# Differential attention: three score regions, alternating row halves, and turned weights through one bank

## The chip, the cores and the metric

One core of a Trainium2 chip runs the whole program. The metric is device time in microseconds (us), the median of several executions. The engines are TensorE (PE for matmuls, PEld for weight loads), VectorE (DVE), ScalarE (ACT), GpSimd (POOL) and SyncE (SP), each with an instruction stream of its own.

## The reference, cut to what matters

Two transformer blocks run one after the other on 512 tokens of width 1024, in float32. The change is in the second block's differential attention: 4 heads, each with two maps of 64 channels, 512 queries, 768 keys (256 of context) and 128 value channels.

```python
def diff_attention(q, k_all, v_all, lam):
    s = jnp.einsum('bhmqd,bhmkd->bhmqk', q, k_all).astype(jnp.float32) * ATTN_SCALE
    pr = jax.nn.softmax(s, axis=-1)
    a = pr[:, :, 0] - lam * pr[:, :, 1]
    return jnp.einsum('bhqk,bhke->bhqe', a.astype(v_all.dtype), v_all)
```

Each head's output is then divided by its root mean square (diff_post).

## The kernel before, in words

The program is a list of phases, and each phase gives every engine a piece of code; phases follow on each engine without a common stop. `diff_attention` comes after `diff_projection` and before `diff_post`. PSUM has eight banks of 512 float32 columns.

The work is cut into 16 **units** (head h, block i of 128 queries), in one loop over u on each engine; the code's order is the order of each engine's queue, and semaphores join the queues.

- TensorE, `scores(pe, u, m)`: the scores of map m, 128x768, are one 512-column and one 256-column matmul. Map 0 lies in partitions 0 to 63 of Q and K, map 1 in 64 to 127, so each uses one half of the array's rows. Map 0 is issued whole, then map 1 (lines 2331 and 2332). Map m has banks 2m and 2m+1, so the scores of unit u wait for the exponential of unit u-1 of the same map (`raised`). In the trace a float32 matmul is two instructions.
- VectorE takes each map's row maximum (line 2380), negates it in a second instruction (2381) and signals `maxed`. After the maxima of unit u it finishes unit u-1: reciprocal of the second map's sum (2387), the ratio (2388), and the difference of the two maps over 768 columns (2389), which signals `ready`.
- ScalarE raises each map (2411), with the row sum read out by a second instruction, and signals `raised`; then it copies (2419) the turned weights of unit u-2 to the table PT and signals `copied`.
- TensorE, `turns(pe, u)`: six transposes of 128x128 (2340) turn the weights of unit u-2 into banks 4 and 5; they wait for `ready` and for the copy of the unit before. `values(pe, h, keys)`: once four units of a head are copied, six key blocks of 512 columns (2349) add up in bank 6, two blocks in each of three units; the head's values begin at u = 4h+6. VectorE takes the result (`take`, 2401), ScalarE squares it (2429), and `diff_sum` (318 and 2445) adds up columns in bank 7.
- While the last units drain, `latents` (2465) fills TensorE with matmuls of the next projection: "context" and "first" at u = 16, "last" after the loop. Then come diff_sum(2), values(3) with all six blocks, and the next phase's products (2135).

Of the kernel before, what the change touches and what calls it, by code (L numbers as in the profile page):

```python
# [16 lines left out]
ALU = mybir.AluOpType  # L17
ACT = mybir.ActivationFunctionType
AX_X = mybir.AxisListType.X

P = 128
D = 1024
KD = D // P
S = 512
# [106 lines left out]
def view(M, off, *dims):  # L131
    n = int(np.prod(dims))
    v = M[:, off:off + n]
    if len(dims) == 1:
        return v
    names = "abcde"[:len(dims)]
    return v.rearrange("p (" + " ".join(names) + ") -> p " + " ".join(names),
                       **{c: d for c, d in zip(names[1:], dims[1:])})
# [1151 lines left out]
class Seven:  # L1290
# [68 lines left out]
    def copy(self, act, u):  # L1359
        self.wait_product(act, u, 1)  # L1360
        if u >= 1:
            self.wait_added(act, u - 1, "u2")
        act.activation(self.CP[:, 0, :], self.bank(1), ACT.Copy).then_inc(self.copied, 1)
# [944 lines left out]
def diff_attention(k):  # L2308


    M = k.M
    Q, K, V = view(M, D_Q, 4, S), view(M, D_K, 4, T_ALL), view(M, D_V, TT, 512)
    MIX, SQ = view(M, A_MIX, KD, S), view(M, D_SQ, 4, S)
    PT, PR = view(M, D_PT, 2, TT, S), view(M, D_P, 3, 2, T_ALL)
    top, total, ratio, floor = view(M, O_SML, 2, 2), view(M, O_SML + 4, 4, 2, 4), view(M, O_SML + 36, 2), view(M, O_SML + 40, 4, 4)
    units = [(h, i) for h in range(4) for i in range(4)]
    N = len(units)
    scored, maxed, raised, ready, turned, copied, valued, taken = (
        k.attention[x] for x in ("scored", "maxed", "raised", "ready", "turned", "copied", "valued", "taken"))
    m0, t0, u0, h0 = (k.attention_count[x] for x in ("scored", "turned", "copied", "valued"))  # L2320
    score = lambda m: k.psum[:, 1024 * m:1024 * m + T_ALL]
    TURN, VALUE = 4, 6
    k.latents = k.sem("latents")
    k.diffpost = squared, summed, rooted, inverted = [k.sem(f"diffpost_{x}") for x in ("squared", "summed", "rooted", "inverted")]

    def scores(pe, u, m):
        h, i = units[u]
        if u >= 1:
            pe.wait_ge(raised, m0 + 2 * u - 1 + m)
        r = slice(64 * m, 64 * m + 64)  # L2330
        pe.matmul(k.bank[2 * m], Q[r, h, i * P:(i + 1) * P], K[r, h, 0:512], start=True, stop=True)  # L2331
        pe.matmul(k.bank[2 * m + 1][:, :256], Q[r, h, i * P:(i + 1) * P], K[r, h, 512:768], start=True,
                  stop=True).then_inc(scored, 1)

    def turns(pe, u):
        pe.wait_ge(ready, u + 1)
        if u >= 1:
            pe.wait_ge(copied, u0 + u)
        for j in range(TT):
            mm = pe.transpose(k.bank[TURN + j // 4][:, (j % 4) * P:(j % 4 + 1) * P], PR[:, u % 3, 0, j * P:(j + 1) * P], k.ident)  # L2340
        mm.then_inc(turned, 1)

    def values(pe, h, keys):
        if 0 in keys:
            pe.wait_ge(copied, u0 + 4 * h + 4)
            if h >= 1:
                pe.wait_ge(taken, h0 + h)
        for j in keys:
            mm = pe.matmul(k.bank[VALUE], V[:, j, h * P:(h + 1) * P], PT[:, h % 2, j, :], start=j == 0, stop=j == TT - 1)  # L2349
        if TT - 1 in keys:  # L2350
            mm.then_inc(valued, 1)

    def tensor(k, pe):
        for u in range(N + 2):
            if u < N:
                scores(pe, u, 0)
            h, step = (u - 2) // 4 - 1, (u - 2) % 4
            if u < N:
                scores(pe, u, 1)
            if h >= 0 and step < 3:  # L2360
                values(pe, h, (2 * step, 2 * step + 1))
            if u == N:
                latents(k, pe, "context")
            if u >= 2:
                turns(pe, u - 2)
            if u % 4 == 3 and u >= 11:
                diff_sum(k, pe, u // 4 - 2)
            if u == N:
                latents(k, pe, "first")
        latents(k, pe, "last")  # L2370
        diff_sum(k, pe, 2)
        values(pe, 3, range(TT))

    def vector(k, dve):
        for u in range(N + 1):
            if u < N:
                for m in range(2):
                    t = top[:, u % 2, m:m + 1]
                    dve.wait_ge(scored, m0 + 2 * u + m + 1)
                    k.dve.link(dve.tensor_reduce(t, score(m), AX_X, ALU.max))  # L2380
                    dve.tensor_scalar(t, t, -1.0, None, ALU.mult).then_inc(maxed, 1)
            if u >= 1:
                v = u - 1
                h, i = units[v]
                r, pr = ratio[:, v % 2:v % 2 + 1], PR[:, v % 3]
                dve.wait_ge(raised, m0 + 2 * v + 2)
                k.dve.link(dve.reciprocal(r, total[:, h, 1, i:i + 1]))
                k.dve.link(dve.scalar_tensor_tensor(out=r, in0=total[:, h, 0, i:i + 1], scalar=k.lam, in1=r, op0=ALU.mult, op1=ALU.mult))
                dve.scalar_tensor_tensor(out=pr[:, 0, :], in0=pr[:, 1, :], scalar=r, in1=pr[:, 0, :],
                                         op0=ALU.mult, op1=ALU.subtract).then_inc(ready, 1)  # L2390
                if i == 3:
                    k.dve.link(dve.tensor_scalar(floor[:, h, :], total[:, h, 0, :], SUBLN_EPS * P / D, None, ALU.mult))
                    k.dve.link(dve.tensor_tensor(floor[:, h, :], floor[:, h, :], total[:, h, 0, :], ALU.mult))
                if u % 4 == 1 and u >= 9:
                    take(dve, u // 4 - 2)
        take(dve, 2)
        take(dve, 3)

    def take(dve, h):
        dve.wait_ge(valued, h0 + h + 1)  # L2400
        dve.tensor_copy(MIX[:, 4 + h, :], k.bank[VALUE]).then_inc(taken, 1)

    def scalar(k, act):
        for u in range(N + 2):
            if u < N:
                if u >= 3:
                    act.wait_ge(turned, t0 + u - 2)
                h, i = units[u]
                for m in range(2):
                    act.wait_ge(maxed, m0 + 2 * u + m + 1)  # L2410
                    act.activation(PR[:, u % 3, m, :], score(m), ACT.Exp, bias=top[:, u % 2, m:m + 1],
                                   accum_out=total[:, h, m, i:i + 1]).then_inc(raised, 1)
            if u >= 2:
                v = u - 2
                h, i = units[v]
                act.wait_ge(turned, t0 + v + 1)
                if h >= 2:
                    act.wait_ge(valued, h0 + h - 1)
                act.activation(PT[:, h % 2, :, i * P:(i + 1) * P],
                               k.psum[:, 512 * TURN:512 * TURN + T_ALL].rearrange("p (j q) -> p j q", q=P),  # L2420
                               ACT.Copy).then_inc(copied, 1)
                if u % 4 == 2 and u >= 10:
                    square(act, u // 4 - 2)
        square(act, 2)
        square(act, 3)

    def square(act, h):
        act.wait_ge(taken, h0 + h + 1)
        act.activation(SQ[:, h, :], MIX[:, 4 + h, :], ACT.Square).then_inc(squared, 1)

    ph = Phase("diff_attention", tensor=tensor, vector=vector, scalar=scalar)
    ph.soft = True
    return ph
# [15 lines left out]
def latents(k, pe, what):  # L2449

    W, A, C = view(k.M, A_MIX, KD, 160), view(k.M, A_A, KD, S), k.ctxT
    raised, m0 = k.attention["raised"], k.attention_count["raised"]
    if what == "gate":
        pe.wait_ge(raised, m0 + 32)
        block_feature(pe, k.bank[2][0:96, :], W, 64, 96, lambda q: A[:, q, :], KD).then_inc(k.latents, 1)
        return
    if what == "context":
        pe.wait_ge(raised, m0 + 31)  # L2460
    bank, rhs, chunks = {"context": (k.bank[1][:, :NC_CTX], C, range(KD)), "first": (k.bank[0], A, range(0, KD // 2)),
                         "last": (k.bank[0], A, range(KD // 2, KD))}[what]
    for q in chunks:
        for r, c0 in ((0, 0), (64, 32)):
            mm = pe.matmul(bank[r:r + 32, :], W[:, q, c0:c0 + 32], rhs[:, q, :], start=q == 0, stop=q == KD - 1)
    if what == "last":
        mm.then_inc(k.latents, 1)
# [1103 lines left out]
```

## Time and profile before

| | us |
|---|---|
| median of 3 runs | 2581.02 |
| lowest, highest run | 2575.54, 2581.93 |
| span of the profiled execution, first to last instruction | 2573.8 |
| first score matmul | 1507.03 |
| first matmul of the next phase (products) | 1603.52 |

The profiled execution has no device time beside its span: the three runs are other executions, and their median lies 7.2 us above the span. The profile gives each instruction's start from the start of the span. PEclk is the granted TensorE clock as a share of 2.4 GHz: 0.50 is its lower level, 1.2 GHz. Matmuls are pipelined, so a matmul's duration includes its drain, and the distance of two starts says how fast they follow.

### The profile page before, as it was taken

To read this page: it belongs to the slowest core of one execution; us is meant where nothing else is said; L and a number is where in the kernel's file an instruction comes from. 1 tells how busy PE (TensorE), PEld (TensorE's weight loads), DVE (VectorE), ACT (ScalarE), POOL (GpSimd) and SP (SyncE) were. 2 spreads that over 40 slices of the span, in tenths; PEclk is the share of its full clock that TensorE was granted. 3 is DMA by queue.
4 is the path that set the end of the run, shared out by engine and by line. 5 is a ranking of instruction groups with operands and counts; after the bars stand their busy time and mean duration, and the time that the engine had idled before them with its cause. 6 is when DMAs were issued, how large, how long until landed. Compare 5 with 4: busy or idle time off the path is not lost.

```text
span 2573.8 us, 45719 instructions
## 1 busy us (share of the span) xinstructions
PE 2460.1 (96%) x19672; PEld 1922.6 (75%) x19672; DVE 1364.2 (53%) x2613; ACT 519.6 (20%) x1046; POOL 127.6 (5%) x106
## 2 busy tenths in 40 slices
PE   8999999999999999999998999998889898999998
PEld 5945888888686548888885664557888746888887
DVE  5636555533454426555435465566666436787633
ACT  2121010000003421010001034224444223112101
POOL 0000000000000000000000000002222200000000
PEclk9999999999999999999999989999999998999999
DMA  5323332233222023232234210400000033223132
GB/s 171 123 84 129 99 98 67 78 90 111 67 66 67 1 66 119 78 98 81 75 90 145 74 33 2 120 1 3 4 4 4 4 112 117 67 98 99 52 84 78
DMA packets 222176, 190.31 MB, mean 74 GB/s; under 512 B 8711, under 2 KB 220072, under 8 KB 221976
## 3 DMA queue, kind: packets, MB, share of 16 engines
q1 hardware_dynamic: 221682, 187.29, 23.6%
q8 instruction: 157, 2.57, 0.4%
q14 instruction: 43, 0.35, 0.0%
q10 hardware_dynamic: 294, 0.09, 0.0%
HBM read 185.25 MB, written 2.10 MB: 73 GB/s over the span
## 4 chain that ended last, share of the span: by engine, by line
PE 90%; DVE 5%; issue 2%; ACT 1%; SPq 1%; POOL 1%; DMA 0%; POOLq 0%; DVEq 0%; ACTq 0%
PE psum L1676 31%; PE psum L1897 14%; PE psum L517 7%; PE psum L2780 6%; PE psum L1353 5%; PE psum L1349 4%; PE psum L1136 4%; PE psum L3335 2%; PE psum L1072 1%; PE psum L2787 1%; PE psum L2331 1%; PE psum L2349 1%; PE psum L539 1%; POOL sbuf L432 1%; PE psum L1115 1%
## 5 line engine op out<-in xcount | busy, mean ns | idle before, releaser
L1676 PE MATMUL psum<-sbuf 128*128 128x256 f32 x3696 | 806.0, 381 | 3.5 <-DVE sbuf L481 1.9
L1676 PEld LDWEIGHTS psum<-sbuf 128*128 128x128 f32 x3696 | 707.1, 191 | 102.1 <-issue 3.1
L1897 PE MATMUL psum<-sbuf 128*128 128x256 f32 x1716 | 370.9, 379 | 0.0
L1897 PEld LDWEIGHTS psum<-sbuf 128*128 128x128 f32 x1716 | 326.0, 190 | 44.3
L1760 DVE TENSOR_TENSOR sbuf<-sbuf,psum 128x256 f32<-128x256 f32 x462 | 177.6, 416 | 202.0 <-PE psum L1676 200.8
L2780 PE MATMUL psum<-sbuf 64*64 64x64 f32 (+1 forms) x5952 | 209.0, 223 | 29.9 <-DVE sbuf L3172 10.2
L2780 PEld LDWEIGHTS psum<-sbuf 64*64 64x64 f32 x5952 | 194.4, 136 | 43.5 <-issue 23.4
L517 PE MATMUL psum<-sbuf 128*128 128x512 f32 (+3 forms) x560 | 205.5, 524 | 0.3 <-issue 0.3
L517 PEld LDWEIGHTS psum<-sbuf 128*128 128x128 f32 (+2 forms) x560 | 104.5, 188 | 93.0 <-issue 87.0
L1933 DVE TENSOR_TENSOR sbuf<-sbuf,psum 128x256 f32<-128x256 f32 x84 | 34.0, 418 | 216.5 <-PE psum L1897 216.1
L432 POOL TENSOR_TENSOR sbuf<-sbuf 128x512 f32<-128x512 f32 x30 | 37.8, 1280 | 1885.9 <-DVE sbuf L418 1885.7
L1353 PE MATMUL psum<-sbuf 128*128 128x256 f32 (+2 forms) x536 | 122.3, 389 | 0.0
L1353 PEld LDWEIGHTS psum<-sbuf 128*128 128x128 f32 x536 | 99.1, 190 | 23.5 <-issue 3.2
L1349 PEld LDWEIGHTS psum<-sbuf 128*128 128x128 f32 x1008 | 113.8, 192 | 2.8 <-issue 2.4
L1136 PE MATMUL psum<-sbuf 128*128 128x512 f32 x256 | 114.3, 595 | 0.6 <-DVEq L622 0.6
L1349 PE MATMUL psum<-sbuf 128*128 128x128 f32 x1008 | 113.8, 275 | 0.0
L1696 ACT ACTIVATE sbuf<-sbuf 128x512 f32<-128x512 f32 x44 | 27.7, 630 | 399.9 <-DVE sbuf L1760 399.9
L3237 POOL TENSOR_TENSOR sbuf<-sbuf 128x512 f32<-128x512 f32 x60 | 75.0, 1274 | 547.4 <-DVE sbuf L3161 517.0
L1411 DVE TENSOR_TENSOR sbuf<-sbuf,psum 128x256 f32<-128x256 f32 (+1 forms) x119 | 53.4, 450 | 70.9 <-PE psum L1353 39.5
L1746 DVE TENSOR_TENSOR sbuf<-sbuf 128x512 f32<-128x512 f32 x66 | 44.4, 689 | 81.2 <-PE psum L1676 67.2
L1136 PEld LDWEIGHTS psum<-sbuf 128*128 128x128 f32 x256 | 46.8, 190 | 51.9 <-issue 51.2
L3172 DVE TENSOR_TENSOR sbuf<-sbuf,psum 128x256 f32<-128x256 f32 x120 | 47.5, 402 | 64.0 <-PE psum L2780 63.8
(281 smaller groups left out, 2653.7 us busy)
## 6 DMA issues: line engine op xcount, KB each, us to landing
sbuf<-in_w_mod_dram SPq DMA_DIRECT2D x24, 1024.0 KB, 5.1
sbuf<-in_w_ffn_gate_dram SPq DMA_DIRECT2D x22, 1024.0 KB, 5.5
sbuf<-in_w_ffn_up_dram SPq DMA_DIRECT2D x22, 1024.0 KB, 7.8
sbuf<-in_w_ffn_down_dram SPq DMA_DIRECT2D x32, 704.0 KB, 5.9
sbuf<-in_w_up_dram SPq DMA_DIRECT2D x22, 1024.0 KB, 7.4
sbuf<-in_w_out_dram SPq DMA_DIRECT2D x12, 1024.0 KB, 6.7
sbuf<-in_w_in_dram SPq DMA_DIRECT2D x12, 1024.0 KB, 5.6
sbuf<-in_w_down_dram SPq DMA_DIRECT2D x16, 704.0 KB, 6.4
```

The source lines that it names most:

```text
L432: pool.tensor_tensor(k.H[:, c, :], k.H[:, c, :], j.tmp[:, n % 3, :], ALU.add).then_inc(j.moved, 1)
L517: mm = pe.matmul(bank, w[:, q, c0:c0 + m], rhs(k0 + q), start=start and q == 0, stop=stop and q == kc - 1)
L1136: mm = pe.matmul(bank_of(b), tiles[b // 2][:, q, (b % 2) * P:(b % 2) * P + P], MIX[:, q, :], start=q == 0, stop=q == KD - 1)
L1349: mm = pe.matmul(self.bank(p)[:, t * P:(t + 1) * P], x[:, q, :], w[:, q, :], start=q == 0, stop=q == 3)
L1353: mm = pe.matmul(self.bank(p)[:, c0:c1], w[:, q, :], x[:, q, :], start=q == 0, stop=q == 3)
L1411: dve.tensor_tensor(out, base, flat(self.bank(p)), ALU.add).then_inc(self.added, 1)
L1676: mm = pe.matmul(bank, w[:, q, :], rhs[:, q, :], start=q == 0, stop=q == 3)
L1760: dve.tensor_tensor(out, base, bank_of(u, p, t), ALU.add).then_inc(s["added"], 1)
L1897: mm = pe.matmul(bank_of(g, p), wt[:, q, :], rhs_of[p][:, q, :], start=q == 0, stop=q == UNITS - 1)
L2780: mm = pe.matmul(out[h], lhsT[h], rhs[h], start=start, stop=stop)
L3237: pool.tensor_tensor(split(LOFF[lv]), split(GB[g % 2][:, :, 0, :]), both_level(lv), ALU.mult).then_inc(sems["loff"], 1)
L3335: mm = pe.matmul(block_bank(b), tiles[b // 2][:, q, (b % 2) * P:(b % 2 + 1) * P], MIX[:, q, :], start=q == order(b)[0], stop=q == order(b) ...
```

## The change

- **Regions.** Six banks in three pairs are handed round: the 2u+m-th map takes pair (2u+m) mod 3. One wait, for the first exponential of unit u-1, goes ahead of both maps' scores, and the four matmuls alternate: both maps' 512 columns, then both maps' 256.
- **Negation.** The maximum is negated in the reduction (`negate=True`); the second instruction and the wait between go.
- **Turned weights.** They pass through bank 7 alone, in two parts: early (key blocks 0 to 3) and late (4 and 5). Each part waits on TensorE for the copy of the part before. ScalarE copies the late part of unit u-3 between the two exponentials of unit u, and the early part of u-2 behind the second.
- **SBUF.** First maps take four buffers, second maps two (six of 768 columns, as before).
- **Shifts.** The values of a head begin one unit later (u = 4h+7), `take` and `square` too; diff_sum(0) to diff_sum(2) all come behind values(3).

```diff
@@ -2311,38 +2311,44 @@
     M = k.M
     Q, K, V = view(M, D_Q, 4, S), view(M, D_K, 4, T_ALL), view(M, D_V, TT, 512)
     MIX, SQ = view(M, A_MIX, KD, S), view(M, D_SQ, 4, S)
-    PT, PR = view(M, D_PT, 2, TT, S), view(M, D_P, 3, 2, T_ALL)
+    PT, PR = view(M, D_PT, 2, TT, S), view(M, D_P, 6, T_ALL)
+    raised_map = lambda u, m: PR[:, u % 4 if m == 0 else 4 + u % 2, :]
...
-    score = lambda m: k.psum[:, 1024 * m:1024 * m + T_ALL]
-    TURN, VALUE = 4, 6
+    region = lambda u, m: 2 * ((2 * u + m) % 3)
+    score = lambda u, m: k.psum[:, 512 * region(u, m):512 * region(u, m) + T_ALL]
+    TURN, VALUE = 7, 6
+    early, late = range(0, 4), range(4, TT)
+    of_turn = lambda u, part: 2 * u + (1 if part is early else 2)
...
 
-    def scores(pe, u, m):
+    def scores(pe, u):
         h, i = units[u]
         if u >= 1:
-            pe.wait_ge(raised, m0 + 2 * u - 1 + m)
-        r = slice(64 * m, 64 * m + 64)
-        pe.matmul(k.bank[2 * m], Q[r, h, i * P:(i + 1) * P], K[r, h, 0:512], start=True, stop=True)
-        pe.matmul(k.bank[2 * m + 1][:, :256], Q[r, h, i * P:(i + 1) * P], K[r, h, 512:768], start=True,
-                  stop=True).then_inc(scored, 1)
-
-    def turns(pe, u):
+            pe.wait_ge(raised, m0 + 2 * u - 1)
+        for keys in (slice(0, 512), slice(512, 768)):
+            for m in range(2):
+                r = slice(64 * m, 64 * m + 64)
+                mm = pe.matmul(score(u, m)[:, keys], Q[r, h, i * P:(i + 1) * P], K[r, h, keys], start=True, stop=True)
+                if keys.stop == T_ALL:
+                    mm.then_inc(scored, 1)
+
+    def turns(pe, u, part):
         pe.wait_ge(ready, u + 1)
-        if u >= 1:
-            pe.wait_ge(copied, u0 + u)
-        for j in range(TT):
-            mm = pe.transpose(k.bank[TURN + j // 4][:, (j % 4) * P:(j % 4 + 1) * P], PR[:, u % 3, 0, j * P:(j + 1) * P], k.ident)
+        if of_turn(u, part) >= 2:
+            pe.wait_ge(copied, u0 + of_turn(u, part) - 1)
+        for j in part:
+            mm = pe.transpose(k.bank[TURN][:, (j - part[0]) * P:(j - part[0] + 1) * P], raised_map(u, 0)[:, j * P:(j + 1) * P], k.ident)
         mm.then_inc(turned, 1)
 
     def values(pe, h, keys):
         if 0 in keys:
-            pe.wait_ge(copied, u0 + 4 * h + 4)
+            pe.wait_ge(copied, u0 + of_turn(4 * h + 3, late))
             if h >= 1:
                 pe.wait_ge(taken, h0 + h)
         for j in keys:
@@ -2352,24 +2358,24 @@
 
     def tensor(k, pe):
         for u in range(N + 2):
+            h, step = (u - 3) // 4 - 1, (u - 3) % 4
             if u < N:
-                scores(pe, u, 0)
-            h, step = (u - 2) // 4 - 1, (u - 2) % 4
-            if u < N:
-                scores(pe, u, 1)
+                scores(pe, u)
+            if u >= 3:
+                turns(pe, u - 3, late)
+            if u == N:
+                latents(k, pe, "context")
             if h >= 0 and step < 3:
                 values(pe, h, (2 * step, 2 * step + 1))
-            if u == N:
-                latents(k, pe, "context")
             if u >= 2:
-                turns(pe, u - 2)
-            if u % 4 == 3 and u >= 11:
-                diff_sum(k, pe, u // 4 - 2)
+                turns(pe, u - 2, early)
             if u == N:
                 latents(k, pe, "first")
         latents(k, pe, "last")
-        diff_sum(k, pe, 2)
+        turns(pe, N - 1, late)
         values(pe, 3, range(TT))
+        for h in range(3):
+            diff_sum(k, pe, h)
 
     def vector(k, dve):
         for u in range(N + 1):
@@ -2377,21 +2383,19 @@
                 for m in range(2):
                     t = top[:, u % 2, m:m + 1]
                     dve.wait_ge(scored, m0 + 2 * u + m + 1)
-                    k.dve.link(dve.tensor_reduce(t, score(m), AX_X, ALU.max))
-                    dve.tensor_scalar(t, t, -1.0, None, ALU.mult).then_inc(maxed, 1)
+                    dve.tensor_reduce(t, score(u, m), AX_X, ALU.max, negate=True).then_inc(maxed, 1)
             if u >= 1:
                 v = u - 1
                 h, i = units[v]
...
...
-                if u % 4 == 1 and u >= 9:
+                if u % 4 == 2 and u >= 10:
                     take(dve, u // 4 - 2)
         take(dve, 2)
         take(dve, 3)
@@ -2401,26 +2405,36 @@
         dve.tensor_copy(MIX[:, 4 + h, :], k.bank[VALUE]).then_inc(taken, 1)
 
     def scalar(k, act):
+        def raise_map(u, m):
+            h, i = units[u]
+            act.wait_ge(maxed, m0 + 2 * u + m + 1)
+            if m == 0 and u >= 4:
+                act.wait_ge(turned, t0 + of_turn(u - 4, late))
+            elif m == 1 and u >= 2:
+                act.wait_ge(ready, u - 1)
+            act.activation(raised_map(u, m), score(u, m), ACT.Exp, bias=top[:, u % 2, m:m + 1],
+                           accum_out=total[:, h, m, i:i + 1]).then_inc(raised, 1)
+
+        def copy(v, part):
+            h, i = units[v]
+            act.wait_ge(turned, t0 + of_turn(v, part))
+            if h >= 2:
+                act.wait_ge(valued, h0 + h - 1)
+            act.activation(PT[:, h % 2, part[0]:part[-1] + 1, i * P:(i + 1) * P],
+                           k.bank[TURN][:, 0:len(part) * P].rearrange("p (j q) -> p j q", q=P), ACT.Copy).then_inc(copied, 1)
+
         for u in range(N + 2):
             if u < N:
-                if u >= 3:
-                    act.wait_ge(turned, t0 + u - 2)
-                h, i = units[u]
-                for m in range(2):
-                    act.wait_ge(maxed, m0 + 2 * u + m + 1)
-                    act.activation(PR[:, u % 3, m, :], score(m), ACT.Exp, bias=top[:, u % 2, m:m + 1],
-                                   accum_out=total[:, h, m, i:i + 1]).then_inc(raised, 1)
+                raise_map(u, 0)
+            if u >= 3:
+                copy(u - 3, late)
+            if u < N:
+                raise_map(u, 1)
             if u >= 2:
-                v = u - 2
-                h, i = units[v]
-                act.wait_ge(turned, t0 + v + 1)
-                if h >= 2:
-                    act.wait_ge(valued, h0 + h - 1)
-                act.activation(PT[:, h % 2, :, i * P:(i + 1) * P],
-                               k.psum[:, 512 * TURN:512 * TURN + T_ALL].rearrange("p (j q) -> p j q", q=P),
-                               ACT.Copy).then_inc(copied, 1)
-                if u % 4 == 2 and u >= 10:
-                    square(act, u // 4 - 2)
+                copy(u - 2, early)
+            if u % 4 == 3 and u >= 11:
+                square(act, u // 4 - 2)
+        copy(N - 1, late)
         square(act, 2)
         square(act, 3)
```

One unit on TensorE, from the scores of a unit whose step has values to the next scores. Before:

```order
L2331 MATMUL psum<-sbuf 128x512 [waits attention_raised]
L2332 MATMUL psum<-sbuf 128x256
L2331 MATMUL psum<-sbuf 128x512 [waits attention_raised]
L2332 MATMUL psum<-sbuf 128x256
L2349 MATMUL psum<-sbuf 128x512 x2
L2340 MATMUL psum<-sbuf 128x128 [waits attention_copied,attention_ready]
L2340 MATMUL psum<-sbuf 128x128 x5
L2331 MATMUL psum<-sbuf 128x512 [waits attention_raised]
```

Now:

```order
L2337 MATMUL psum<-sbuf 128x512 [waits attention_raised]
L2337 MATMUL psum<-sbuf 128x512
L2337 MATMUL psum<-sbuf 128x256 x2
L2346 MATMUL psum<-sbuf 128x128 [waits attention_copied,attention_ready]
L2346 MATMUL psum<-sbuf 128x128
L2355 MATMUL psum<-sbuf 128x512 x2
L2346 MATMUL psum<-sbuf 128x128 [waits attention_copied,attention_ready]
L2346 MATMUL psum<-sbuf 128x128 x3
L2337 MATMUL psum<-sbuf 128x512 [waits attention_raised]
```

The 512-column matmuls of both maps stand together. The six transposes stand in two groups around the values, and each group waits for a copy.

The same unit on ScalarE, two units long. Before:

```order
L2411 ACTIVATE sbuf<-psum,sbuf 128x768 [waits attention_maxed,attention_turned]
L2411 ACTIVATE sbuf<-psum,sbuf 128x768 [waits attention_maxed]
L2419 ACTIVATE sbuf<-psum 128x6x128 [waits attention_turned]
L2411 ACTIVATE sbuf<-psum,sbuf 128x768 [waits attention_maxed,attention_turned]
L2411 ACTIVATE sbuf<-psum,sbuf 128x768 [waits attention_maxed]
L2419 ACTIVATE sbuf<-psum 128x6x128 [waits attention_turned]
```

Now:

```order
L2415 ACTIVATE sbuf<-psum,sbuf 128x768 [waits attention_turned,attention_maxed]
L2423 ACTIVATE sbuf<-psum 128x2x128 [waits attention_turned]
L2415 ACTIVATE sbuf<-psum,sbuf 128x768 [waits attention_ready,attention_maxed]
L2423 ACTIVATE sbuf<-psum 128x4x128 [waits attention_turned]
L2415 ACTIVATE sbuf<-psum,sbuf 128x768 [waits attention_turned,attention_maxed]
L2423 ACTIVATE sbuf<-psum 128x2x128 [waits attention_turned]
L2415 ACTIVATE sbuf<-psum,sbuf 128x768 [waits attention_ready,attention_maxed]
L2423 ACTIVATE sbuf<-psum 128x4x128 [waits attention_turned]
```

The copy of six blocks behind both exponentials has become a copy of two blocks between them and one of four behind them.

The end of the stage on TensorE, from the turns of unit 15 (before):

```order
L2340 MATMUL psum<-sbuf 128x128 [waits attention_copied,attention_ready]
L2340 MATMUL psum<-sbuf 128x128 x5
L2465 MATMUL psum<-sbuf 32x512 x8
L318 MATMUL psum<-sbuf 32x128 [waits diffpost_squared]
L318 MATMUL psum<-sbuf 32x128 x3
L2445 MATMUL psum<-sbuf 32x128 x4
L2349 MATMUL psum<-sbuf 128x512 [waits attention_taken,attention_copied]
L2349 MATMUL psum<-sbuf 128x512 x5
L2135 MATMUL psum<-sbuf 2x256 [waits tile_landed2,tile_landed3,tile_landed1,tile_landed0]
L2135 MATMUL psum<-sbuf 2x256 x31
```

Now, from the late turns of unit 14:

```order
L2346 MATMUL psum<-sbuf 128x128 [waits attention_copied,attention_ready]
L2346 MATMUL psum<-sbuf 128x128
L2355 MATMUL psum<-sbuf 128x512 x2
L2346 MATMUL psum<-sbuf 128x128 [waits attention_copied,attention_ready]
L2346 MATMUL psum<-sbuf 128x128 x3
L2479 MATMUL psum<-sbuf 32x512 x8
L2346 MATMUL psum<-sbuf 128x128 [waits attention_copied,attention_ready]
L2346 MATMUL psum<-sbuf 128x128
L2355 MATMUL psum<-sbuf 128x512 [waits attention_taken,attention_copied]
L2355 MATMUL psum<-sbuf 128x512 x5
L318 MATMUL psum<-sbuf 32x128 [waits diffpost_squared]
L318 MATMUL psum<-sbuf 32x128 x3
```

A pair of value blocks and the late turns of unit 15 now come in the last stretch; values(3) follow these turns directly. The products (2135) now follow two more groups of 318 and 2459.

## Rows read from the trace of the kernel before

**Rows 1.** The page's chain that ended last: shares of the span by engine.

```profile
PE 90%; DVE 5%; issue 2%; ACT 1%; SPq 1%; POOL 1%; DMA 0%; POOLq 0%; DVEq 0%; ACTq 0%
```

**Rows 2.** Windows: us, PE, PEld, DVE, ACT, POOL busy, PEclk, DMA share, GB/s.

```profile
1512.40:1526.10 13.70, 13.36 (x33) 6.67 (x30) 9.03 (x17) 5.43 (x10) 0.00 (x0) 0.50 0.00 0
1526.10:1553.40 27.30, 24.53 (x103) 13.05 (x102) 22.57 (x52) 17.89 (x35) 0.00 (x0) 1.00 0.00 1
1553.40:1560.20 6.80, 6.80 (x15) 2.95 (x13) 4.05 (x9) 2.35 (x5) 0.00 (x0) 0.50 0.00 0
1560.20:1582.50 22.30, 21.31 (x105) 11.83 (x104) 16.89 (x37) 13.94 (x26) 0.00 (x0) 1.00 0.00 1
```

**Rows 3.** Timeline of unit 7: start, us, engine, line, operation [idle before <- releaser].

```profile
1539.25 1.14 PE L2331 MATMUL psum<-sbuf 64*128 64x512 f32 x4
...
1540.75 1.98 PE L2349 MATMUL psum<-sbuf 128*128 128x512 f32 x4
1540.84 0.96 DVE L2380 TENSOR_REDUCE sbuf<-psum 128x1 f32<-128x768 f32 x1 [1.47 <-PE psum L2332]
1541.28 0.19 PEld L2349 LDWEIGHTS psum<-sbuf 128*128 128x128 f32 x1 [0.24 <-issue]
1541.71 0.19 PEld L2349 LDWEIGHTS psum<-sbuf 128*128 128x128 f32 x1 [0.24 <-issue]
1541.84 0.15 DVE L2381 TENSOR_SCALAR sbuf<-sbuf 128x1 f32<-128x1 f32 x1
1541.91 0.95 DVE L2380 TENSOR_REDUCE sbuf<-psum 128x1 f32<-128x768 f32 x1
1542.09 0.90 ACT L2411 ACTIVATE sbuf<-psum,sbuf 128x768 f32<-128x768 f32 x1 [1.92 <-DVE sbuf L2381]
...
1542.57 0.82 PE L2340 MATMUL psum<-sbuf 128*128 128x128 f32 x6
...
1542.88 0.19 ACT L2411 ACTIVATION_READ_ACCUMULATOR sbuf<-psum,sbuf 128x1 f32 x1
...
1543.08 0.90 ACT L2411 ACTIVATE sbuf<-psum,sbuf 128x768 f32<-128x768 f32 x1
...
1543.32 1.50 PE L2331 MATMUL psum<-sbuf 64*128 64x512 f32 x3
```

**Rows 4.** Timeline, first exponential's end in unit 9 and scores of unit 10.

```profile
1551.88 0.19 ACT L2411 ACTIVATION_READ_ACCUMULATOR sbuf<-psum,sbuf 128x1 f32 x1
...
1552.12 1.12 PE L2331 MATMUL psum<-sbuf 64*128 64x512 f32 x2 [1.57 <-ACT sbuf L2411]
```

**Rows 5.** Timeline of VectorE: first map's reduction of units 1, 4, 6, 10, 11, 12.

```profile
1512.66 0.96 DVE L2380 TENSOR_REDUCE sbuf<-psum 128x1 f32<-128x768 f32 x1 [1.75 <-PE psum L2332]
...
1527.97 0.96 DVE L2380 TENSOR_REDUCE sbuf<-psum 128x1 f32<-128x768 f32 x1 [0.30 <-PE psum L2332]
...
1535.80 0.96 DVE L2380 TENSOR_REDUCE sbuf<-psum 128x1 f32<-128x768 f32 x1 [0.30 <-PE psum L2332]
...
1553.93 0.95 DVE L2380 TENSOR_REDUCE sbuf<-psum 128x1 f32<-128x768 f32 x1
...
1562.10 0.96 DVE L2380 TENSOR_REDUCE sbuf<-psum 128x1 f32<-128x768 f32 x1 [3.71 <-PE psum L2332]
...
1566.74 0.96 DVE L2380 TENSOR_REDUCE sbuf<-psum 128x1 f32<-128x768 f32 x1 [1.06 <-PE psum L2332]
```

**Rows 6.** Three lines of the program: durations in ns, minimum/median/maximum.

```profile
L2155 ACT ACTIVATE sbuf<-psum x6: 366/367/385, 141.8 to 2144.8; 98x256 f32<-98x256 f32 x6
...
L2491 ACT ACTIVATE sbuf<-psum x1: 597/597/597, 1609.1 to 1609.1; 128x512 f32<-128x512 f32 x1
...
L2340 PE MATMUL psum<-sbuf x96: 272/273/473, 1519.7 to 1593.5; 128*128 128x128 f32 x96
```

**Rows 7.** Timeline of TensorE from the last scores to the next phase.

```profile
1578.42 1.16 PE L2331 MATMUL psum<-sbuf 64*128 64x512 f32 x4
...
1582.51 0.42 PE L318 MATMUL psum<-sbuf 128*32 128x128 f32 x8
...
1583.08 1.98 PE L2349 MATMUL psum<-sbuf 128*128 128x512 f32 x4
...
1603.52 3.63 PE L2135 MATMUL psum<-sbuf 128*2 128x256 f32 x64 [0.37 <-issue]
```

More of the change, by code:

```diff
@@ L2384, in vector @@
                 h, i = units[v]
-                r, pr = ratio[:, v % 2:v % 2 + 1], PR[:, v % 3]
+                r, one, two = ratio[:, v % 2:v % 2 + 1], raised_map(v, 0), raised_map(v, 1)
                 dve.wait_ge(raised, m0 + 2 * v + 2)
@@ L2388, in vector @@
                 k.dve.link(dve.scalar_tensor_tensor(out=r, in0=total[:, h, 0, i:i + 1], scalar=k.lam, in1=r, op0=ALU.mult, op1=ALU.mult))
-                dve.scalar_tensor_tensor(out=pr[:, 0, :], in0=pr[:, 1, :], scalar=r, in1=pr[:, 0, :],
-                                         op0=ALU.mult, op1=ALU.subtract).then_inc(ready, 1)
+                dve.scalar_tensor_tensor(out=one, in0=two, scalar=r, in1=one, op0=ALU.mult, op1=ALU.subtract).then_inc(ready, 1)
                 if i == 3:
```

## The prediction

> **What bounds the kernel now.** I began with the chain that ended last [rows 1]: TensorE holds 90% of it over the whole kernel, so what moves the attention stage's last matmul moves the end. The stage is 96 of 2573.8 us, first score at 1507.03, next phase's first matmul at 1603.52 [rows 2, 7]. The stage by stretches [rows 2] shows what the share hides: TensorE's granted clock is 0.50 from 1512.40 to 1526.10 and again from 1553.40 to 1560.20, 20.5 us in all, and 1.00 in the rest. VectorE is busy 22.57 of 27.30 us in the middle stretch, ScalarE 17.89: neither is full.
>
> One unit in order of time [rows 3] then shows a loop over three engines. From the first score matmul (1539.25) to the first map's maximum (1540.84) are 1.59 us; from there to the exponential (1542.09) 1.25 us, since reduction (0.96), negation (0.15) and hand-overs follow each other; exponential and read of its sum hold ScalarE until the second map's exponential (1543.08), 0.99 us; 0.05 us later the scores of the next unit may start (sum read out at 1551.88 + 0.19, scores at 1552.12 [rows 4]). That makes 3.88 us, and two units without values took 1535.80 - 1527.97 = 7.83 us, 3.92 each [rows 5]: there the loop binds. With values TensorE's own queue binds: 1566.74 - 1562.10 = 4.64 us [rows 5].
>
> **The change, term by term** (full clock first).
>
> *Negation.* Gone from the loop: 1.25 becomes 0.96 + 0.09 = 1.05 us (0.09 is the gap from the negation's end, 1541.84 + 0.15, to 1542.09, rounded). The trace has no negated reduction; I take its time as the plain one's. If it costs as much as reduction and negation together, the 0.20 returns, 3 us over 15 periods. A gain above 0.20 is excluded, as the reduction still reads 768 columns.
>
> *Alternating maps.* The four 512-column matmuls of both maps already take 1.14 us [rows 3], against 1.12 us for two of one map [rows 4]: the halves of the array run side by side even though the program issues one map after the other. Nothing saved on the first map, on which the loop turns. The Trainium skill (TensorE: Matmul & The Clock Gate, The mechanism) says that matmuls keep strict program order in start and end; by that, alternating them would win one map's matmuls in every unit. This trace disagrees, by the 1.14 us just read.
>
> *Turned weights through one bank.* This puts a link into the loop. On TensorE a unit is now: scores, two late turns of unit u-3, values, four early turns of unit u-2. The early turns write the bank that holds the late ones, so they wait for the copy of the late part; ScalarE issues that copy behind the first exponential of unit u. Queued behind the early turns on TensorE are the scores of unit u+1, and maxima and exponentials wait for those. From the first score: 1.59 + 1.05 + 0.99, then the copy of 256 columns, the hand-over, and four turns. The copy: 98x256 took 0.37 and 128x512 0.60 [rows 6]; I take 0.39, near the row of its width, and 0.60 is the upper end. Hand-over to TensorE: 0.10, twice the 0.05 read above since two semaphores are waited for. Six turns up to the next score took 1543.32 - 1542.57 = 0.75, at 0.11 a turn (0.82 less the last one's 0.27, by five [rows 3, 6]); four take 0.53. Sum 4.65 us per unit, in place of 3.92 without values and about 4.6 with them. Values and late turns lie in the wait for the copy and cost nothing: scores 1.5 (1539.25 to 1540.75), late turns 0.3 and values 1.8 (1540.75 to 1542.57) end at 3.6, and the copy is there at 4.1.
>
> *Sum to the last unit's scores.* Three first periods have no early turn behind a copy: 1.59 + 1.05 + 0.99 + 0.05 = 3.68 each, 11.0; twelve of 4.65 make 55.8. From 1507.03 the last unit's scores then start at 1573.9, against 1578.42 [rows 7]: 4.5 earlier, if the clock were full throughout.
>
> *The tail.* Before, 25.1 us (1603.52 - 1578.42) lie between these scores and the next phase. From the end of the early turns of unit 13 (4.65 us after the scores; before, turns of 13 and diff_sum(1) end as late, 1583.08 - 1578.42 = 4.66) the new order adds: a wait for the early copy, which stands behind the second exponential (3.63 + 0.39 + 0.99 + 0.60 + 0.10 = 5.7, so 1.07); two late turns 0.35; one more pair of value blocks, as the values now lag by one unit, 1.8; at the end the late copy of unit 15, which values(3) wait for with nothing left to do in between: drain 0.27, copy 0.39, hand-overs 0.19, 0.85; two more of the three diff_sum now lie here, 1583.08 - 1582.51 = 0.57 each [rows 7], 1.14. Together +5.2. So +0.7 at full clock.
>
> *The clock.* Half clock cost before: three periods in 1527.97 - 1512.66 = 15.3 us rather than 11.8, and one in 8.17 (1553.93 to 1562.10) rather than 4.64 [rows 5]: 7.1 us. This is already inside 1578.42. The new loop pays for half clock too: scores 1.28 and turns 0.5 more, 1.8 us per period, only 1.3 in the first two. TensorE works less in it (1.9 of 4.65 us without values, where the old one had the maps staggered), and before, 1.57 us of idle preceded the fall at 1553.40 [rows 2, 4]. Lower bound: no half clock, 0. Upper bound: half clock up to unit 7, where values begin, 2.6 + 4 x 1.8 = 9.8, and one fall at each of the two later units without values, 2 x 3.5: 16.8. I take the first stretch as ending half-way (2.6 + 3.6 = 6.2) and one later fall at even odds (1.8): 8.0.
>
> Sum: 0.7 + 8.0 = **+8.7 us**. The profiled execution has a span of 2573.8; 7.2 us lie between that and the median of 2581.02, taken as constant, and the three runs spread over 6.4 us. 2581.0 + 8.7 = 2589.7. Later phases are paced by TensorE and move as they are.
>
> **Rivals.**
> - *Clock full throughout*: for it, values and scores alternate evenly from unit 7; against it, fewer busy halves before that. 2581.0 + 0.7 = 2581.7.
> - *Half clock for longer*, its upper bound: 2581.0 + 17.5 = 2598.5.
> - *Scores pass the waiting turns* (faster): the second map's matmuls got ahead of the first's in [rows 3]. If the next scores could pass early turns that wait for the copy, the period would be 3.68 without values and TensorE's own 1.5 + 0.3 + 1.8 + 0.5 = 4.1 with them: last scores at 1507.0 + 9 x 3.68 + 6 x 4.1 = 1564.7, 13.7 earlier, tail +5.2: 2572.5. It decides from the point where a score starts before the early turns ahead of it. Against: turns use all 128 rows and the wait stands ahead in the same queue.
> - *The halves ran apart until now* (faster): if alternation alone made the maps run together, one map's 1.28 us (a 512-column matmul takes 0.43, weight loads at 1541.28 and 1541.71 [rows 3], half that for 256 columns, two of each) would go in 16 units: 2589.7 - 20.5 = 2569.2. The skill's rule above would give this. The 1.14 us speaks against it.
> - *Delay absorbed*: a later wait (weights for the next projection) hides it: 2581. Against: that phase's loads are released by the same TensorE work.
>
> **How the numbers follow.** Forecast 0.50, with an own range of 2584 to 2596 (copy 0.39 to 0.60 adds 2.5, the clock term +-4); full clock 0.18; longer half clock 0.15; passing 0.06; halves apart 0.04; absorbed 0.07. 0.3% (7.7 us) is about what a measurement of this kernel can tell from no change. Of the forecast's 0.50, 0.12 lie below 2588.7. Slower: 0.38 + 0.15 = 0.53. Same: 0.12 + 0.18 + 0.07 = 0.37. Faster: 0.10. The range runs from 2579 to 2598, leaving out the faster cases and about half of the longest.
>
> **What would show it.** In the profile after: early turns starting about 0.1 us behind a 256-column copy in nearly every unit; maxima 4.6 to 4.7 us apart at full clock with and without values, 6 to 6.5 at half; four 512-column score matmuls still in 1.14 us, but now in every unit; 0.8 us of idle ahead of the last values; the next phase's matmuls some 8 to 9 us later than 1603.5. It is wrong if a period without values stays under 4 us, or if the granted clock in the stage is 1.00.

## The result and the profile after

| | before | after |
|---|---|---|
| median, us | 2578.38 (20 runs) | 2582.07 (20 runs) |
| lowest to highest | 2574.44 to 2584.75 | 2577.38 to 2588.43 |
| ratio, 95% interval | | 1.0017 (1.0010 to 1.0024) |
| span of the profiled execution | 2573.8 | 2575.6 |
| first score to products (the stage) | 1507.03 to 1603.52: 96.5 | 1505.00 to 1605.28: 100.3 |

The changed kernel is slower by 3.7 us between the medians (its ratio of 1.0017 would be 4.4 us), less than half of what was forecast and inside the bound of 0.3%. The stage is 3.8 us longer in the profiled executions. What comes before it differs by 2.0 us the other way (first score at 1505.00 against 1507.03) and what follows takes 970.3 us in both, so in these two profiles only the stage got longer. Equal to a tenth is luck: in the profiles of the experiments 970.8 to 978.3 us follow the stage. One profile per kernel fixes the loop's periods well, and a difference of kernel times only to some us.

One unit at full clock in the timeline of the profile after; columns as in [rows 3], matmuls that follow each other without a gap merged:

```profile
1547.18 1.56 PE L2337 MATMUL psum<-sbuf 64*128 64x512 f32 x8
...
1548.68 0.44 PE L2346 MATMUL psum<-sbuf 128*128 128x128 f32 x2
...
1548.85 1.82 DVE L2386 TENSOR_REDUCE sbuf<-psum 128x1 f32<-128x768 f32 x2 [1.15 <-PE psum L2337]
1548.95 1.88 PE L2355 MATMUL psum<-sbuf 128*128 128x512 f32 x4
...
1549.84 0.90 ACT L2415 ACTIVATE sbuf<-psum,sbuf 128x768 f32<-128x768 f32 x1 [1.95 <-DVE sbuf L2386]
...
1550.64 0.19 ACT L2415 ACTIVATION_READ_ACCUMULATOR sbuf<-psum,sbuf 128x1 f32 x1
1550.73 0.37 ACT L2423 ACTIVATE sbuf<-psum 128x256 f32<-128x256 f32 x1
...
1551.25 0.63 PE L2346 MATMUL psum<-sbuf 128*128 128x128 f32 x4 [0.41 <-ACT sbuf L2423]
...
1551.80 1.56 PE L2337 MATMUL psum<-sbuf 64*128 64x512 f32 x8
```

This is the forecast's chain, link by link: score to maximum 1.67 us (forecast 1.59), maximum to exponential 0.99 (1.05), exponential to copy 0.89 (0.99), copy 0.37 (0.39), hand-over 0.15 (0.10), early turns to the next scores 0.55 (0.53). TensorE has done the values by 1550.8 and waits 0.41 us for ScalarE's copy. The sum is 4.62, from these scores to the next. The distance of two first maxima is 4.55 or 4.62 at full clock, with values and without them, where [rows 5] has 3.92 without.

TensorE in the end of the stage, the same view, beside [rows 7]:

```profile
1579.78 0.63 PE L2346 MATMUL psum<-sbuf 128*128 128x128 f32 x4
1581.19 0.41 PE L2346 MATMUL psum<-sbuf 128*128 128x128 f32 x2 [0.78 <-ACT sbuf L2423]
1581.53 3.65 PE L2479 MATMUL psum<-sbuf 128*32 128x256 f32 x32
...
1597.10 0.44 PE L2346 MATMUL psum<-sbuf 128*128 128x128 f32 x2
1598.02 5.42 PE L2355 MATMUL psum<-sbuf 128*128 128x512 f32 x12 [0.47 <-ACT sbuf L2423]
1603.36 0.43 PE L318 MATMUL psum<-sbuf 128*32 128x128 f32 x8
...
1603.82 0.40 PE L318 MATMUL psum<-sbuf 128*32 128x128 f32 x8
...
1605.28 1.05 PE L2135 MATMUL psum<-sbuf 128*2 128x256 f32 x16 [0.40 <-issue]
```

Both waits of the forecast's tail stand in brackets, 0.78 and 0.47 us; the next phase begins 1.8 us later than in the profile before, not 8 to 9.

The granted clock by windows, the four stretches at half clock (columns as in [rows 2]):

```profile
1510.00:1516.90 6.90, 4.55 (x16) 1.90 (x12) 4.43 (x7) 2.18 (x5) 0.00 (x0) 0.51 0.00 0
1527.10:1530.50 3.40, 2.88 (x10) 0.98 (x6) 1.20 (x3) 0.40 (x2) 0.00 (x0) 0.50 0.00 0
1537.30:1540.80 3.50, 3.50 (x11) 1.51 (x8) 1.19 (x2) 0.57 (x2) 0.00 (x0) 0.51 0.00 0
1574.90:1578.30 3.40, 3.40 (x11) 1.55 (x10) 1.49 (x3) 0.44 (x1) 0.00 (x0) 0.50 0.02 5
```

17.2 us in four pieces, where the forecast's middle value had one stretch up to about unit 5 and half of a later one. The clock falls four times instead of twice, and its stretches at half clock are 6.9 us and three of 3.4 or 3.5, where they were 13.7 and 6.8. In the units without values TensorE idles about 2 us ahead of the early turns, and then early turns, both maps' scores and late turns follow without a gap. TensorE in units 4 and 5, across the fall at 1527.1:

```profile
1521.63 0.63 PE L2346 MATMUL psum<-sbuf 128*128 128x128 f32 x4 [2.06 <-ACT sbuf L2423]
1522.19 1.56 PE L2337 MATMUL psum<-sbuf 64*128 64x512 f32 x8
1523.68 0.44 PE L2346 MATMUL psum<-sbuf 128*128 128x128 f32 x2
1526.19 0.63 PE L2346 MATMUL psum<-sbuf 128*128 128x128 f32 x4 [2.07 <-ACT sbuf L2423]
1526.74 2.62 PE L2337 MATMUL psum<-sbuf 64*128 64x512 f32 x8
```

The same scores take 1.56 us and then 2.62. The same idle time stood ahead of both, so these rows do not say when the clock falls.

### The profile page after: what moved, and what is told of

It is laid out like the page before. It is cut to its first block, busy times and chain, and to the rows that moved or that the text cites. A ratio compares the mean times of both kernels' runs of the same rounds, so it can differ in the third digit from the quotient of the medians.

```text
span 2575.6 us, 45740 instructions
## 1 busy us (share of the span) xinstructions
PE 2445.0 (95%) x19672; PEld 1911.3 (74%) x19672; DVE 1359.8 (53%) x2581; ACT 518.8 (20%) x1062; POOL 127.5 (5%) x106
## 4 chain that ended last, share of the span: by engine, by line
PE 89%; DVE 5%; issue 2%; ACT 1%; SPq 1%; POOL 1%; DMA 0%; POOLq 0%; DVEq 0%; ACTq 0%
PE psum L1676 31%; PE psum L1897 14%; PE psum L517 7%; PE psum L2794 6%; PE psum L1353 5%; PE psum L1349 4%; PE psum L1136 4%; PE psum L3349 2%; PE psum L2337 1%; PE psum L2801 1%; PE psum L1072 1%; PE psum L539 1%; POOL sbuf L432 1%; PE psum L1115 1%; PE psum L1868 1%
```

## Experiments

Ten kernels ran. In the ratios the kernel before, measured beside each of them again, is 1. The medians of different rows were not all measured side by side, so small differences between rows are better read from the ratios.

| kernel | edit | median us | ratio (95%) | stage us |
|---|---|---|---|---|
| e1 | changed, late copy first | 2572.35 | 0.9979 (0.9969 to 0.9988) | 88.3 |
| e2 | changed, map 0 whole, then map 1 | 2584.74 | 1.0024 (1.0015 to 1.0034) | 103.1 |
| e4 | changed, negation apart | 2590.22 | 1.0045 (1.0032 to 1.0057) | 108.5 |
| e5 | changed, idle time filled | 2580.99 | 1.0009 (1.0000 to 1.0018) | 97.8 |
| e3 | before, negated reduction | 2572.16 | 0.9972 (0.9961 to 0.9983) | 90.3 |
| e6 | e1 and two moves at the end | 2568.22 | 0.9956 (0.9940 to 0.9971) | 86.8 |
| e7 | e6, start filled | 2565.61 | 0.9946 (0.9931 to 0.9962) | 85.2 |
| e8 | changed, late copy last | 2598.51 (2 runs) | 1.0074 (1.0047 to 1.0102) | 115.1 |
| e9 | changed, again | 2581.86 | 1.0020 (1.0011 to 1.0029) | 103.0 |
| e10 | e2, again | 2581.49 | 1.0021 (1.0011 to 1.0030) | 103.0 |

### e1: the link taken away

```diff
         for u in range(N + 2):
-            if u < N:
-                raise_map(u, 0)
             if u >= 3:
                 copy(u - 3, late)
+            if u < N:
+                raise_map(u, 0)
             if u < N:
                 raise_map(u, 1)
```

> The changed kernel with one edit: ScalarE copies the late part of unit u-3 ahead of the first exponential of unit u, not between the two. Theory A (the copy behind the first exponential is the link of the loop): the late turns are done about 1.9 us after the first score, the copy by 2.5, before the exponential can start (2.65), so the early turns wait for nothing; the distance of two maxima of the first map falls from 4.56 to about 3.7 without values and 4.1 with them, the stage (100.3 us from the first score to the products) to 88 to 93, the kernel to 0.3 to 0.45% below the changed one and 0.1 to 0.3% below the one before. Theory B (TensorE and the half clock set the stage): the distances stay at 4.5, the stage at 98 to 101.

Measured: 0.9979, 5.8 us below before and 9.7 below the changed kernel; stage 88.3 us. Its timeline from unit 7's early turns on, TensorE and ScalarE:

```profile
1540.02 0.60 PE L2346 MATMUL psum<-sbuf 128*128 128x128 f32 x4
...
1540.55 1.56 PE L2337 MATMUL psum<-sbuf 64*128 64x512 f32 x8
...
1542.04 0.44 PE L2346 MATMUL psum<-sbuf 128*128 128x128 f32 x2
1542.14 1.82 DVE L2386 TENSOR_REDUCE sbuf<-psum 128x1 f32<-128x768 f32 x2 [0.82 <-PE psum L2337]
1542.32 1.88 PE L2355 MATMUL psum<-sbuf 128*128 128x512 f32 x4
1542.52 0.38 ACT L2423 ACTIVATE sbuf<-psum 128x256 f32<-128x256 f32 x1 [1.04 <-PE psum L2346]
1543.13 0.90 ACT L2415 ACTIVATE sbuf<-psum,sbuf 128x768 f32<-128x768 f32 x1 [0.23 <-DVE sbuf L2386]
...
1544.04 0.60 PE L2346 MATMUL psum<-sbuf 128*128 128x128 f32 x4
...
1544.57 1.56 PE L2337 MATMUL psum<-sbuf 64*128 64x512 f32 x8
...
1551.08 0.63 PE L2346 MATMUL psum<-sbuf 128*128 128x128 f32 x4 [0.56 <-ACT sbuf L2423]
```

The copy now starts 0.6 us ahead of the exponential and fits into ScalarE's idle time. The early turns follow the values without a wait (1544.04), and the next scores follow them (1544.57), so TensorE's queue is the bound where values lie. The distance between first maxima is 3.63 us without values and up to 4.14 with them. Theory A stands in periods, stage and time. In a unit without values the early turns still wait for the copy (0.56 us at 1551.08), but the period stays at that of the kernel without this link. The half clock also shrinks, to one stretch of 6.8 us at the start. The first two periods take 4.18 and 5.00 us where 3.63 is full clock, 1.9 us more, and the changed kernel's half clock costs 5.0 by the same count (worked out further down). So of the 12.0 us between the two stages about 3 are the clock's and 9 the link's.

### e8: the link made longer

Edit: `copy(u - 3, late)` goes behind `raise_map(u, 1)`.

> The changed kernel with the wait lengthened: the late copy goes behind the second exponential too. Theory A (link): the period at full clock grows by one exponential, from 4.56 to about 5.5 us, with and without values, the stage by 12 us or more. Rival: no change.

```profile
1559.07 1.82 DVE L2386 TENSOR_REDUCE sbuf<-psum 128x1 f32<-128x768 f32 x2 [2.02 <-PE psum L2337]
1564.51 1.82 DVE L2386 TENSOR_REDUCE sbuf<-psum 128x1 f32<-128x768 f32 x2 [2.24 <-PE psum L2337]
1569.94 1.82 DVE L2386 TENSOR_REDUCE sbuf<-psum 128x1 f32<-128x768 f32 x2 [1.64 <-PE psum L2337]
```

VectorE's maxima are 5.44 and 5.43 us apart: 4.55 and one exponential of 0.89. The stage is 14.8 us longer. Twelve longer periods and one exponential in the tail are some 11.5 of it; the rest is half clock, 27.3 us of it in this stage against 17.2. e1, the changed kernel and e8 differ in the place of one copy in ScalarE's queue and give 3.6 to 4.1, 4.6 and 5.4 us per unit.

### e2, e9 and e10: alternating row halves

```diff
-        for keys in (slice(0, 512), slice(512, 768)):
-            for m in range(2):
-                r = slice(64 * m, 64 * m + 64)
+        for m in range(2):
+            r = slice(64 * m, 64 * m + 64)
+            for keys in (slice(0, 512), slice(512, 768)):
```

> The changed kernel with the four score matmuls in the old order, map 0 whole and then map 1; all waits as they are. Theory A (the halves of the array run side by side in either order): all four 512-column score instructions of a unit start within 0.6 us, stage and kernel as the changed one within 1 us. Rival (matmuls keep program order, so alternating is what lets them run together): the second map starts 1.28 us behind the first, the second maximum too, stage 100.3 + 0 to 20 us.

The periods at full clock were the same (3.63, 4.55 and 4.62), but the stage was 103.1 us, not within 1 us of 100.3, and the median was 2.7 us above the changed kernel's, which had not been measured beside it. So both ran once more, side by side:

> The changed kernel once more, beside the same kernel with map 0 whole and then map 1, on one chip. Theory A (the order of the score matmuls changes nothing; the 2.7 us between their medians are spread of the half clock): the medians lie within 1.5 us of each other. Rival (alternating wins something): this one 2 to 3 us faster again.

> The changed kernel with map 0 whole and then map 1, once more. Theory A: within 1.5 us of the changed kernel's median of this call. Rival: 2 to 3 us slower.

Measured: 2581.86 and 2581.49, 0.4 us apart. One unit's eight score matmuls in e10, and below them those among the eight that start before 1549.5:

```profile
1548.81 1.57 PE L2337 MATMUL psum<-sbuf 64*128 64x512 f32 x8
```

```profile
1548.81 1.14 PE L2337 MATMUL psum<-sbuf 64*128 64x512 f32 x4
```

1.57 us for both maps issued one after the other, and 1.56 alternated (above). Though map 0's 256 columns stand ahead of map 1's 512 in e10's program, the four instructions of 512 columns run first, both maps' together. The alternation is worth nothing that these runs can tell: the 2.7 us did not come again. Windows over the whole stage, e9 and then e10:

```profile
1508.00:1611.00 103.00, 81.94 (x384) 37.99 (x384) 53.84 (x93) 45.65 (x100) 0.00 (x0) 0.88 0.03 11
```

```profile
1508.40:1611.40 103.00, 82.06 (x384) 38.35 (x385) 53.84 (x93) 45.63 (x100) 0.00 (x0) 0.88 0.03 11
```

The same program as in the profile after takes 103.0 instead of 100.3 us here, at a mean clock of 0.88 against 0.91: its full-clock periods are the same, only the half clock holds for longer (23.9 us, in five stretches).

### e4 and e3: the negation

```diff
-                    dve.tensor_reduce(t, score(u, m), AX_X, ALU.max, negate=True).then_inc(maxed, 1)
+                    k.dve.link(dve.tensor_reduce(t, score(u, m), AX_X, ALU.max))
+                    dve.tensor_scalar(t, t, -1.0, None, ALU.mult).then_inc(maxed, 1)
```

> The changed kernel with reduction and negation as two instructions again. Theory A (the loop goes through the first maximum in every unit): each period 0.2 us longer, 4.76, the stage 3 us longer, kernel 0.1% above the changed one. Rival (VectorE or TensorE binds, the maximum has slack): no change, within 1 us.

e3 is the reverse edit in the kernel before.

> The kernel before with one part of the change: the maximum is negated in the reduction. Theory A (the first maximum lies in the old loop too, where no values bind): 0.2 us less in about 7 of 15 periods and in the two with half clock, 1.5 to 3 us in all, 0.05 to 0.12% faster. Rival (in the old kernel the shorter loop changes the half-clock time as well, as the longer one did in the new kernel): 3 to 8 us either way.

VectorE in e4:

```profile
1550.49 0.96 DVE L2386 TENSOR_REDUCE sbuf<-psum 128x1 f32<-128x768 f32 x1 [1.16 <-PE psum L2337]
1551.48 0.15 DVE L2387 TENSOR_SCALAR sbuf<-sbuf 128x1 f32<-128x1 f32 x1
...
1555.30 0.96 DVE L2386 TENSOR_REDUCE sbuf<-psum 128x1 f32<-128x768 f32 x1 [0.96 <-PE psum L2337]
...
1560.04 0.96 DVE L2386 TENSOR_REDUCE sbuf<-psum 128x1 f32<-128x768 f32 x1 [1.16 <-PE psum L2337]
```

4.81 and 4.74 us apart against 4.62 and 4.55: 0.19 per period, 2.9 in the stage, as theory A says. But the kernel lost 8 us, not its 0.1%: the stage now has 30.7 us at half clock, in five pieces. Its whole stage in one window:

```profile
1506.30:1614.80 108.50, 83.96 (x388) 38.54 (x392) 58.73 (x125) 45.99 (x100) 0.00 (x0) 0.86 0.03 10
```

Windows of e3:

```profile
1509.50:1550.00 40.50, 33.87 (x143) 18.00 (x144) 30.41 (x51) 24.00 (x48) 0.00 (x0) 1.00 0.08 26
1550.00:1556.90 6.90, 6.90 (x15) 3.04 (x14) 3.97 (x7) 2.56 (x5) 0.00 (x0) 0.51 0.00 0
1556.90:1599.80 42.90, 41.64 (x231) 19.68 (x231) 18.97 (x35) 16.98 (x31) 0.00 (x0) 1.00 0.00 1
```

The first stretch of [rows 2], 13.7 us at half clock, is not there. e3's 0.28% are the rival's size and above theory A's 0.12%: for a step of 0.2 us, 7 us. This profile is of the slowest of e3's twelve executions (2579.91); what it took longer lies behind the stage, 978.3 us for 970.3. The clock of all executions says the same as the windows: its mean over the whole kernel was 0.983 in e3's, 0.981 in those of the kernel before beside them, and 0.979 in e4's for 0.982 in the changed kernel's. The negated reduction itself takes no longer than the plain one (two in 1.82 us). So the negation is worth 7 to 8 us in either kernel, and the rest of the change, which is what e4 has, costs 0.45%. Next to e3, e1 says what that rest is: with the negation and without the link it stands at 0.9979, with the negation alone at 0.9972, and the two intervals overlap. Regions, alternation and shifts together are worth nothing that these runs can tell; no run has the three regions by themselves.

### e5 and e7: the idle time filled

Both add matmuls whose result is overwritten by the next unit's scores; nothing of the computation is left out.

```diff
             if h >= 0 and step < 3:
                 values(pe, h, (2 * step, 2 * step + 1))
+            elif 2 <= u < N - 1:
+                pe.wait_ge(raised, m0 + 2 * u)
+                for n in range(2):
+                    pe.matmul(score(u + 1, 0)[:, 0:512], V[:, n, 0:P], V[:, n, :], start=True, stop=True)
```

> The changed kernel with work added: in the nine units up to 14 that have no values, TensorE gets two 512-column float32 matmuls (1.7 us at full clock) into the score region that the next unit's scores overwrite, where it now idles for the copy. Theory A (the loop binds, and the idle time of these units is what lets the granted clock fall): periods stay at 4.56, no half clock in the stage once the filling starts, stage 3 to 4 us shorter than the changed one's 100.3 in spite of 15 us more of matmuls. Rival (TensorE's time counts): stage longer, up to 115 us. Rival 2 (the clock does not matter): stage the same.

Windows of e5:

```profile
1508.80:1513.90 5.10, 2.79 (x16) 1.38 (x16) 1.82 (x2) 1.87 (x4) 0.00 (x0) 1.00 0.63 206
1513.90:1520.70 6.80, 4.74 (x14) 1.99 (x11) 4.35 (x7) 2.10 (x5) 0.00 (x0) 0.50 0.00 0
1520.70:1606.70 86.00, 79.65 (x391) 36.09 (x393) 47.67 (x85) 41.53 (x92) 0.00 (x0) 1.00 0.00 1
```

Once the filling is under way, from 1520.7 on, the clock stays at 1.00 to the end, all later periods are 4.55 or 4.62, and the stage is 97.8 us: work was added and this stage is shorter. The expected 3 to 4 us are 2.5 against the profile after and 5.2 against e9's. In the kernel's time the gain is not clear of noise: 1.0009 against 1.0017 and 1.0020, with overlapping intervals. The effect on the clock is clearer: its mean over the whole kernel was 0.984 in e5's eleven executions and 0.982 in the changed kernel's twenty.

e7 does it for units 0 to 2 in e6 (`elif u <= 2`).

> The previous kernel with two 512-column matmuls of filling in each of units 0, 1 and 2, into the score region that the next unit overwrites. Theory A (the half clock at the start, 6.8 us in the copy-first kernel's trace, comes from TensorE's idle time between the first units): no half clock in the stage, 2 to 3 us faster than the previous one. Rival (it comes from the phase before): the same half clock, 0 to 1 us slower.

```profile
1504.70:1590.10 85.40, 77.98 (x400) 36.66 (x404) 53.58 (x93) 46.34 (x100) 0.00 (x0) 1.00 0.04 13
```

No half clock is left in the stage (1504.76 to 1589.91, 85.2 us); it is 1.7 us shorter and the median 2.6 us lower, though the two intervals overlap. The last first-map maximum to the products stays at 26.0.

### e6: the end of the stage

```diff
-            if u >= 3:
-                turns(pe, u - 3, late)
             if u == N:
                 latents(k, pe, "context")
+            if u >= 3:
+                turns(pe, u - 3, late)
...
-        latents(k, pe, "last")
+        latents(k, pe, "third")
         turns(pe, N - 1, late)
+        latents(k, pe, "last")
```

"last" is split into two chunks and two chunks.

> The copy-first kernel with two moves at the end of the stage on TensorE: the context latents go ahead of the late turns of unit 13, and the late turns of unit 15 ahead of the last two chunks of the latents. Theory A (both waits for a copy at the end lie on the path): 1.1 and 0.85 us go, from the last maximum to the products 25.6 us in place of 27.6, kernel 0.07% below the copy-first one. Rival (they only move the wait): no change.

From the last first-map maximum to the products: 26.0 us against 27.6, so 1.5 of the expected 1.95 went. e6 is 0.44% faster than before, and e7, the fastest, 0.54%. Against e1 that is 0.23%, where 0.07% was expected: the median fell by 4.1 us, and the stage gives 1.5 of it. The rest is open; the mean granted clock over the whole kernel was 0.985 in e6's seven executions and 0.983 in e1's ten, with the same 6.8 us of half clock in both profiled stages.

## Why the prediction was wrong

The forecast was slower by 8.7 us, 0.34%; measured were 3.7 us between the medians, 0.17% by the ratio. The mechanism, its place and the sign were right: e1 and e8 move it both ways. What failed are the sizes of two terms of the sum: the full-clock sum, +0.7, which measured -1.2, and the clock, 8.0, which measured 5.0 in the profile after. Together they make the stage's 3.8.

- *Sum to the last unit's scores, and tail.* Forecast +0.7 at full clock. With the measured periods, 3 x 3.63 + 9 x 4.55 + 3 x 4.62 = 65.7, 1.7 from first score to first maximum and 27.9 from the last first-map maximum to the products, the stage at full clock is 95.3: -1.2 against 96.5. One us is the period (4.57 on average for 4.65: exponential to copy 0.89 instead of 0.99). The rest, 0.8, is mostly the tail: 1579.78 to 1581.19, 1.41 us, for 0.53 + 1.07; 1597.10 to 1598.02, 0.92, for 0.35 + 0.85; 0.46 per diff_sum, from 1603.36 to 1603.82, instead of 0.57. This miss stands in every profile of the changed kernel, since the periods at full clock do.
- *The clock.* The step is "I take the first stretch as ending half-way ... 8.0". The profile after has 100.3 - 95.3 = 5.0 us of it. A period wholly at half clock was priced at 1.8 us more; the three later stretches, 3.4 us each, were shorter than a period and cost about 1.1 us each, and the one at the start cost 1.7 us, not 6.2. But in e9, the same program, the clock costs 7.7 us, nearly as forecast, and its stage is 6.5 us longer than the one before while the medians differ by 4.8. So the size of this term belongs to the execution, and that the two misses fill the gap so exactly in the profile after is in part luck. Over many executions the clock hardly changed: its mean over the whole kernel was 0.981 in e9's twelve and in the 23 of the kernel before beside them. There is one profile of the kernel before, so what its stage takes in other executions, and with it some 2 to 3 us of the miss, stays open. That filling the idle time keeps the clock up is shown (e5, e7); what makes it fall in one unit and not in the next, and what brings it back, is not.
- *The base.* The span of 2573.8 was that of an execution at the fast end of what turned out to be 2574 to 2585, and so was the after's 2575.6. The 7.2 us "around the span" were mostly this: where runs have both, device time is 1.8 us above the span. The base of 2581.0 was 2.6 us above the later median of 2578.4.
- *Negation.* Its direct term, 0.2 us per period, is exact (e4: 0.19). That it stood for 7 to 8 us by way of the clock was in no term.
- *Alternating maps.* Right: e10 against e9. The strict program order that the Trainium skill states (TensorE: Matmul & The Clock Gate, The mechanism) does not hold here: four 512-column instructions of both maps run in 1.14 us ahead of the 256-column ones, though e10's program has map 0 whole first.
- *Rivals.* Full clock throughout did not come. Its 2581.7 is near the result of 2582.1 by luck: the base was 2.6 us too high and its difference of 0.7 us was 3.0 too low. The longer half clock came in e4, not here. No score passed a waiting turn. Nothing later absorbed the delay in the two profiles: 970.3 us follow the stage in both.

## What to carry to other kernels

When a buffer is handed round in smaller parts, follow each new wait through the order of the queue that answers it. Here one bank for two parts cost nothing per unit with the copy one place earlier on ScalarE; where it stood it cost 0.9 us, an exponential, in a unit without values, and about half of that in one with them. And where TensorE idles in unit after unit, a step of 0.2 us on the loop can be worth several times its sum, by the granted clock (7 to 8 us for 3 here). Price the clock as a range, and take more than one profile before you read its size.

## What the runs showed that was not expected

- More work made the kernel no slower: e5 has some 12 us more of matmuls in the stage (seven units of 1.7 us, not the nine and 15 us of its expectation) and a stage 2.5 us shorter.
- Half clock in the stage differs between executions of the same program, 17.2 us in the profile after and 24 in e9, with 100.3 and 103.0 us for the stage. That is 2.7 us, not much less than the change's whole effect of 3.7, so a pair of single profiles can't size it.
- ScalarE started a copy 0.89 us after an exponential, though the read of the row's sum (0.19 us) lies between: the exponential runs from 1549.84 for 0.90 us, and the read starts at 1550.64, before it ends.
